# GpSimd makes three quarters of the first weight chunk's low halves, VectorE the rest in two pieces

## The chip, the cores and the metric

The kernel runs on one core of a Trainium2 chip. The metric is the device time of one execution in microseconds (us), smaller is better. The kernel before takes 1351.69 us, the median of three runs between 1349.7 and 1352.07 us.

## What is computed

Two transformer-like blocks over 256 positions of width 1024. The first block (gated linear attention beside sparse attention, then a mixture of 16384 experts with 128 chosen per position) ends in a residual sum; the second block opens with a norm and a wide projection.

```python
x = x + gate2 * _peer(h2, ...)          # end of the first block
return _rmsnorm(x, final_norm_g)
...
h = rmsnorm(x, g_mix[i])                # start of the second block
z = jnp.einsum("bsd,dn->bsn", h, w_in[i])
```

The change lies at this seam, in the product `z`.

## The kernel before, in words

**High and low halves.** A product of two 32-bit matrices is made of three passes of TensorE over rounded operands. A weight chunk `whole` is copied by ScalarE into a rounded tile `hi`, and VectorE makes `lo = whole - hi`. The activation is parted likewise (`h_hi` by ScalarE, `h_lo` by VectorE). The passes are hi by h_hi, hi by h_lo and lo by h_hi (`three`, lines 770, 771, 772).

**The chunks of z.** The weights of `z` come in 9 chunks of 128x4096 elements: 8 blocks k of 512 columns, one for each 128 rows of the width. Chunk 0 (`FIRST_C`) is loaded by SyncE in four quarters of 1024 columns (two blocks k each), the others whole. `low` of a chunk lies where `whole` of it lay (`w_lo` is an alias of `raw`), so each subtraction reads and writes in place; both of its inputs are in SBUF.

**Order of work at the seam.** Each engine runs its own stream in order, written out by hand; semaphores join them.

- VectorE: the last two expert rows are added to the sum (`last_row`, four instructions of 128x512), then `expert_x(1, k)` adds the transposed expert sum of the second 128 positions to `xT` (128x128, one input from PSUM, one from SBUF), and `low_of_x(k)` makes `h_lo` of block k (128x256, two inputs from SBUF, line 1917) followed by `expert_x(1, k + 2)`. Between these, `rest_first(q)` (line 2509) makes the low halves of quarter q of chunk 0. After block 7, `rest()` (line 1959) makes the low halves of chunk 1.
- ScalarE: `part_first` (line 1353) rounds quarters 0 and 1 of chunk 0; then for each k it waits for `expert_x(1, k)` and makes `h_hi` of block k (`hi_of_x`, line 1356), with quarters 2 and 3 after k = 1 and 2, and from k = 3 on a square of 128x128 behind each. After k = 7 come three more squares (line 1726) and `part()` (line 1346), the rounding of chunk 1.
- TensorE: `turn_experts(1)` transposes the expert sum (L1093), with unread matmuls between (L1169), and `first_gate` does the 96 matmuls of chunk 0, four banks abreast, block k by block k. Its k = 0 stands on lines 1179 (high by high), 1182 (high by low) and 1185 (low by high); each later k waits for `h_lo` of that block, and k = 2, 4, 6 for the low halves of the next quarter. Then come 16 matmuls of sums of squares (line 1198) and chunk 1 on lines 770 to 772, which waits for the low halves of all of chunk 1.
- GpSimd: it issues the gathers of expert rows (lines 659 and 664). After the last of them its stream is empty.

The semaphore `w_hi` counts rounded chunks and quarters, `w_lo` the low halves made by VectorE; `split_count` gives the count that belongs to a chunk and block.

Of the kernel before, what the change touches and what calls it, by code (L numbers as in the profile page):

```python
# [14 lines left out]
F32 = mybir.dt.float32  # L15
U32 = mybir.dt.uint32
F32R = mybir.dt.float32r
ALU = mybir.AluOpType
# [7 lines left out]
KD = D // P  # L26
# [128 lines left out]
FIRST_C = CHUNK_AT[("z", 0)]  # L155
FIRST_B = BLOCK_AT[("z", 0)]
WHOLE = ("iq", "yb", "ya")
PARTED = [n for n, c in enumerate(CHUNKS) if c[0][0] not in WHOLE]
PARTED_EARLY = len([key for key in EARLY if key[0] not in WHOLE])
# [3 lines left out]
PG = CHUNK_AT[("pg", 0)]  # L163
# [33 lines left out]
def halves(stage, k=0):  # L197

    names = [name for name, _ in HALVES]
    return sum(n for _, n in HALVES[:names.index(stage)]) + k + 1  # L200
# [10 lines left out]
def split_count(c, k=KD - 1):  # L211

    n = PARTED.index(c)
    if n < PARTED_EARLY:
        return n + 1
    at = n + 1 + (k // 2 if n == PARTED_EARLY else KD // 2 - 1)
    return at + (k // 4 if c == PG else n > PARTED.index(PG))


INPUTS = ["dsa_w_uv", "gla_w_gate_up"]  # L220
# [2 lines left out]
def two_blocks(nc, w, out):  # L223
    with ExitStack() as ctx:
        made = {}

        def S(name):

            if name not in made:
                made[name] = ctx.enter_context(nc.semaphore(name))  # L230
            return made[name]
# [32 lines left out]
        def alias(name, start, *dims, dt=F32R):  # L264

            pad = [(name + "_pad", [P, start], F32)] if start else []
            return overlay(*pad, (name, [P, *dims], dt))[-1]
# [30 lines left out]
        def again(start, *dims):  # L298

            at[0] = start  # L300
            return view(*dims)
# [112 lines left out]
        raw, w_lo = again(a_raw, SLOTS, W), alias("w_lo", a_raw, SLOTS, W)  # L414
# [6 lines left out]
        w_hi = alias("w_hi", a_ring, SLOTS, W)  # L421
# [30 lines left out]
        def parts(c):  # L452

            n = CHUNKS[c][2] * CHUNKS[c][5]
            if c in PQ_HOME:
                where, lo, hi, _, _ = PQ_HOME[c]
                return pq_raw[where][:, lo, 0:n], pq_r[where][:, hi, 0:n], pq_r[where][:, lo, 0:n]
            if c < FIRST_C:
                r = c % RAW
                return e_raw[:, r, 0:n], e_hi[:, c % 3, 0:n], e_lo[:, r, 0:n]  # L460
            r, h = (c - FIRST_C) % SLOTS, -(PARTED.index(c) - PARTED_EARLY) % SLOTS
            hi = first_hi if c == FIRST_C else w_hi[:, h, :]
            return raw[:, r, 0:n], hi[:, 0:n], w_lo[:, r, 0:n]

        def by_block(a, n=512):
            return a.rearrange("p (k n) -> p k n", n=n)
# [11 lines left out]
        def quarter(a, q):  # L478
            return a[:, q * QUARTER:(q + 1) * QUARTER]
# [239 lines left out]
            head(N_HEAD - 1, 1, last=True)  # L719


        @block.tensor
        def _(pe):
            done = [0]

            def begin(key):

                n = BLOCK_AT[key]
                assert n == done[0], (key, n, done[0])
                done[0] += 1  # L730
                c = chunk_of(n)
                if key[0] == "down":
                    pass
                elif key[0] == "pl":
                    pe.wait_ge(S("p_in"), 32)
                elif c in PARTED:

                    if c == FIRST_C:
                        pe.wait_ge(S("w_hi"), split_count(c, 0))
                    else:  # L740
                        pe.wait_ge(S("w_lo"), split_count(c, 0 if c == PG else KD - 1))
                else:
                    pe.wait_ge(*arrival(c))
                if BANK_BEFORE[n] is not None:

                    e = BLOCKS[BANK_BEFORE[n]][1]
                    pe.wait_ge(S("taken_" + e), taken_by(e, BANK_BEFORE[n]))
                if key[0] == "pl":
                    return BK[BANK_OF[n]], ple_w
                if c in PARTED:  # L750
                    return BK[BANK_OF[n]], None
                _, _, kt, _, _, nn = CHUNKS[c]
                whole = e_raw[:, c % RAW, 0:kt * nn] if c < FIRST_C else raw[:, (c - FIRST_C) % SLOTS, 0:kt * nn]
                return BK[BANK_OF[n]], whole.rearrange("p (k n) -> p k n", n=nn)
# [23 lines left out]
            def abreast(name, m, x_hi, x_lo, stage, between=None, after=KD - 2, n=T):  # L778


                outs = [begin((name, b))[0][:, 0:n] for b in range(m)]
                for k in range(KD):
                    pe.wait_ge(S("x_lo"), halves(stage, k))
                    if name == "pg" and k == 4:
                        pe.wait_ge(S("w_lo"), split_count(PG, k))
                    for b in range(m):
                        mm = three(outs[b], (name, b), column((name, b)), k, x_hi, x_lo)
                        if k == KD - 1:
                            mm.then_inc(S("product"), 1)
                    if between and k == after:  # L790
                        between()
# [381 lines left out]
            def first_gate():  # L1173

                outs = [begin(("z", b))[0][:, 0:T] for b in range(4)]
                hi, lo = (by_block(a) for a in parts(FIRST_C)[1:])
                pe.wait_ge(S("x_hi"), halves("z", 0))
                for b in range(4):
                    pe.matmul(outs[b], hi[:, 0, b * P:(b + 1) * P], h_hi[:, 0, :], start=True, stop=False, skip_group_check=True)
                pe.wait_ge(S("x_lo"), halves("z", 0))  # L1180
                for b in range(4):
                    pe.matmul(outs[b], hi[:, 0, b * P:(b + 1) * P], h_lo[:, 0, :], start=False, stop=False, skip_group_check=True)
                pe.wait_ge(S("w_lo"), split_count(FIRST_C, 0))
                for b in range(4):
                    pe.matmul(outs[b], lo[:, 0, b * P:(b + 1) * P], h_hi[:, 0, :], start=False, stop=False, skip_group_check=True)
                for k in range(1, KD):
                    pe.wait_ge(S("x_lo"), halves("z", k))
                    if k in (2, 4, 6):
                        pe.wait_ge(S("w_lo"), split_count(FIRST_C, k))
                    for b in range(4):  # L1190
                        mm = three(outs[b], ("z", b), b * P, k, h_hi, h_lo)
                        if k == KD - 1:
                            mm.then_inc(S("product"), 1)
# [53 lines left out]
            for j in range(4):  # L1247
                outs = [begin(("down", 2 * j + b))[0] for b in range(2)]
                for half in range(2):
                    c = CHUNK_AT[("down", j, half)]  # L1250
                    pe.wait_ge(S("w_lo"), split_count(c))
                    hi, lo = (by_block(a, 256) for a in parts(c)[1:])
                    for b in range(2):
                        o, cs = outs[b][:, 0:T], slice(b * P, (b + 1) * P)
                        for k in range(FB // 2):
                            f = half * FB // 2 + k
                            if j == 0 and b == 0:

                                pe.wait_ge(S("f_lo"), f + 1)
                            pe.matmul(o, hi[:, k, cs], f_hi[:, f, :], start=f == 0, stop=False, skip_group_check=True)  # L1260
                            pe.matmul(o, hi[:, k, cs], f_lo(f), start=False, stop=False, skip_group_check=True)  # L1261
                            mm = pe.matmul(o, lo[:, k, cs], f_hi[:, f, :], start=False, stop=f == FB - 1,  # L1262
                                           skip_group_check=True)
                        if half:
                            mm.then_inc(S("product"), 1)
                    if half == 0:
                        mm.then_inc(S("down_half"), 1)
# [639 lines left out]
        def _(v):  # L1907
# [594 lines left out]
            link(v.tensor_tensor(g2e[:, :], cols("final_norm_g", KD), cols("final_norm_g", KD), ALU.mult))  # L2502
            link(v.tensor_scalar(g2e[:, :], g2e[:, :], EPS, None, ALU.add))

            def rest_first(q):

                whole, hi, lo = (quarter(a, q) for a in parts(FIRST_C))
                v.wait_ge(S("w_hi"), split_count(FIRST_C, 2 * q))
                v.tensor_tensor(lo, whole, hi.bitcast(F32), ALU.subtract).then_inc(S("w_lo"), 1)

            link(v.tensor_scalar(half_id[:, 0, :], rowid[:, 1, LAST_J - 1:EK], 1, None, ALU.logical_shift_left))
# [31 lines left out]
            def low_of_x(k):  # L2543
                lo_of_x("z", k, gfm[:, k:k + 1])
                if k + 2 < KD:
                    expert_x(1, k + 2)

            low_of_x(0)
            for q in range(4):
                rest_first(q)  # L2550
                for k in (2 * q + 1, 2 * q + 2):
                    if k < KD:
                        low_of_x(k)
            rest()
            v.wait_ge(S("nm_root"), 1)
            link(v.reciprocal(stat[:, 1, :], tmp))
# [298 lines left out]
```

## Time and profile before

| | |
|---|---|
| median of 3 runs | 1351.69 us |
| profiled execution, its own time | 1353.7 us |
| its span | 1352.0 us |
| TensorE busy, share of the span | 90% |
| VectorE / ScalarE / GpSimd busy | 78% / 46% / 21% |
| mean granted TensorE clock | 0.986 |
| the seam, from the last expert matmuls to chunk 1 of z | some 963 to 984 us from the start |

The profiled execution took 1353.7 us, which is its span of 1352.0 us and 1.7 us around it. Times in the rows are from the start of the span. A row of the timeline gives start, length, engine, line, operation, written tile, read tiles, shapes, and in brackets how long the engine was idle before it and what ended that. The engines' names are PE (TensorE), PEld (its weight loads), DVE (VectorE), ACT (ScalarE) and POOL (GpSimd).

### The profile page before, as it was taken

The numbers are of one execution on the slowest core, as the hardware profiler recorded it, in microseconds if no ns is written. First come the engines' busy times: TensorE is split into PE (matmuls) and PEld (weight loads), VectorE is DVE, ScalarE is ACT, GpSimd is POOL, SyncE is SP. The second block draws the span as 40 slices with busy tenths as digits, with TensorE's granted clock in tenths as the row PEclk, the third lists the DMA queues.
The fourth block names the chain that finished last, engine by engine and source line by source line (L and its number), as shares of the span: only waits on it lengthen the run. The fifth ranks groups of instructions, "written<-read, shape, count | busy, mean of one in ns | idle before, by whom it ended". The sixth has DMA issues, their size and how long they took to land. (4 is left out here: it accounts for less than half of the span.)

```text
span 1352.0 us, 19494 instructions
## 1 busy us (share of the span) xinstructions
PE 1215.2 (90%) x6952; PEld 908.0 (67%) x6952; DVE 1059.7 (78%) x2161; ACT 616.0 (46%) x1265; POOL 290.1 (21%) x280
## 2 busy tenths in 40 slices
PE   7999999999989877778877777787899999999998
PEld 5999999999743333324332232333699999999998
DVE  7898678887879777777766777777699978898666
ACT  4666555656333333332433333233563265554445
POOL 1010000002545544344444434443000000000000
PEclk9999999999999999999999999999999999999999
DMA  9966446665999999999999999999853545454461
GB/s 388 384 225 249 187 158 235 245 234 234 375 422 426 427 428 428 427 427 427 427 427 427 427 428 428 428 427 428 341 187 126 187 137 183 180 187 173 174 236 43
DMA packets 55488, 416.64 MB, mean 308 GB/s; under 512 B 6113, under 2 KB 6753, under 8 KB 9202
## 3 DMA queue, kind: packets, MB, share of 16 engines
q0 software_dynamic: 37152, 268.45, 47.2%
q1 hardware_dynamic: 17792, 146.51, 29.3%
q8 instruction: 50, 0.82, 0.2%
q10 hardware_dynamic: 466, 0.63, 0.1%
q14 instruction: 28, 0.23, 0.0%
HBM read 414.52 MB, written 1.05 MB: 307 GB/s over the span
## 5 line engine op out<-in xcount | busy, mean ns | idle before, releaser
L1109 PE MATMUL ps<-arena 128*128 128x512 f32 x512 | 234.6, 603 | 57.0 <-ACT arena L1613 57.0
L1109 PE MATMUL ps<-ring,arena 128*128 128x512 f32 x440 | 214.1, 637 | 47.1 <-ACT arena L1613 47.1
L2377 DVE CUSTOM_DVE_ANT_0 arena<-arena 128x1024 f32<-128x1024 f32 x128 | 151.7, 1223 | 99.0 <-DMA arena<-in_experts,rowid 96.3
L1109 PEld LDWEIGHTS ps<-arena 128*128 128x128 f32 x512 | 92.7, 189 | 193.9 <-ACT arena L1613 98.0
L659 POOL DMA_INDIRECT arena<-in_experts,rowid x128 | 128.7, 1005 | 351.7 <-DVE rowid L2304 191.0
L1109 PEld LDWEIGHTS ps<-ring,arena 128*128 128x128 f32 x440 | 86.1, 202 | 170.4 <-issue 92.6
L772 PE MATMUL ps<-h_hi,w_lo 128*128 128x256 f32 x700 | 194.9, 278 | 0.0
L1606 ACT ACTIVATE arena<-arena 128x2 f32<-128x2 f32 x126 | 25.6, 203 | 369.1 <-DVE arena L2377 368.9
L770 PE MATMUL ps<-h_hi,w_hi 128*128 128x256 f32 x672 | 189.0, 281 | 3.0 <-DVE w_lo L1959 2.4
L771 PE MATMUL ps<-h_lo,w_hi 128*128 128x256 f32 x672 | 187.2, 279 | 0.0
L2377 DVE CUSTOM_DVE_ANT_0 ring<-ring,arena 128x1024 f32<-128x1024 f32 x112 | 133.3, 1222 | 35.4 <-DMA ring<-in_experts,rowid 26.5
L659 POOL DMA_INDIRECT ring<-in_experts,rowid x110 | 127.1, 1155 | 133.2 <-PE ps L1109 98.9
L1959 DVE TENSOR_TENSOR w_lo<-arena,w_hi 128x4096 fp32r<-128x4096 f32 (+1 forms) x30 | 122.1, 4069 | 29.7 <-ACT w_hi L1346 29.1
L1346 ACT ACTIVATE w_hi<-arena 128x4096 fp32r<-128x4096 f32 (+1 forms) x30 | 100.4, 3346 | 76.2 <-DMA arena<-in_up_w 32.1
L772 PEld LDWEIGHTS ps<-h_hi,w_lo 128*128 128x128 f32 x700 | 132.3, 189 | 0.0
L770 PEld LDWEIGHTS ps<-h_hi,w_hi 128*128 128x128 f32 x672 | 127.3, 190 | 4.1 <-DVE w_lo L1959 3.0
L771 PEld LDWEIGHTS ps<-h_lo,w_hi 128*128 128x128 f32 x672 | 127.1, 189 | 0.2
L770 PE MATMUL ps<-n_hi,e_hi 128*128 128x256 f32 (+1 forms) x352 | 101.4, 288 | 0.2 <-issue 0.2
L771 PE MATMUL ps<-n_lo,e_hi 128*128 128x256 f32 (+1 forms) x352 | 98.1, 279 | 0.0
L772 PE MATMUL ps<-n_hi,e_lo 128*128 128x256 f32 (+1 forms) x352 | 98.1, 279 | 0.0
L1959 DVE TENSOR_TENSOR e_lo<-ring,e_hi 128x2048 fp32r<-128x2048 f32 (+1 forms) x38 | 86.3, 2271 | 11.4 <-ACT e_hi L1346 10.8
L1613 ACT ACTIVATE arena<-ident,arena 128x128 f32<-128x128 f32 x252 | 85.4, 386 | 0.0
(424 smaller groups left out, 2558.4 us busy)
## 6 DMA issues: line engine op xcount, KB each, us to landing
ring<-in_early_w SPq DMA_DIRECT2D x43, 1024.0 KB, 5.0
arena<-in_ada_w SPq DMA_DIRECT2D x24, 1024.0 KB, 8.1
arena<-in_up_w SPq DMA_DIRECT2D x11, 2048.0 KB, 7.8
arena<-in_z_w SPq DMA_DIRECT2D x8, 2048.0 KB, 7.9
arena<-in_down_w SPq DMA_DIRECT2D x8, 1408.0 KB, 6.1
arena<-in_o_w SPq DMA_DIRECT2D x2, 2048.0 KB, 8.1
arena<-in_early_w SPq DMA_DIRECT2D x3, 1024.0 KB, 7.6
arena<-in_experts,rowid POOLq DMA_INDIRECT x128
```

What stands on the lines that cost most here:

```text
L659: pool.indirect_dma_start(out=rows[j], out_offset=None, in_=w["experts"], in_offset=bass.IndirectOffsetOnAxis(ap=rowid[:, even, j:j + 1], ...
L770: pe.matmul(out, hi[:, k, c0:c0 + m], x_hi[:, k, :], start=k == 0, stop=False, skip_group_check=True)
L771: pe.matmul(out, hi[:, k, c0:c0 + m], x_lo[:, k, :], start=False, stop=False, skip_group_check=True)
L772: return pe.matmul(out, lo[:, k, c0:c0 + m], x_hi[:, k, :], start=False, stop=k == KD - 1, skip_group_check=True)
L1109: mm = pe.matmul(BK[4 + 2 * t + b], diag[:, j, :], rows[j][:, D + b * 512:D + (b + 1) * 512], start=first and j == 0, stop=last and j == ( ...
L1346: act.activation(hi, whole, ACT.Copy).then_inc(S("w_hi"), 1)
L1606: act.activation(gel[:, even, two], dots[:, even, two], ACT.Gelu).then_inc(S("act_head"), 1)
L1613: act.activation(diag[:, j, :], ident[:, :], ACT.Copy, scale=amul[:, even, j:j + 1]).then_inc(S("diag"), 1)
L1959: v.tensor_tensor(lo, whole, hi.bitcast(F32), ALU.subtract).then_inc(S("w_lo"), 1)
L2377: v.tensor_tensor_reduce(out=u, in0=u, in1=h2tok[:, t, :], scale=1.0, scalar=0.0, op0=ALU.mult, op1=ALU.add, accum_out=dots[:, even, j:j + ...
```

## The change

GpSimd gets three subtractions behind its last gather: the low halves of quarters 1, 2 and 3 of chunk 0, each after the rounding of its quarter, counted on a new semaphore `first_lo`. VectorE makes quarter 0 only, in two pieces of 512 columns (blocks 0 and 1), each ahead of the `low_of_x` of the next block. TensorE waits for `w_lo` at k = 0 and 1 and for `first_lo` at k = 2, 4, 6. `low_count` corrects the later counts of `w_lo` by two.

```diff
+def low_count(c, k=KD - 1):
+
+    n = PARTED.index(c)
+    if n == PARTED_EARLY:
+        return n + 1 + k
+    return split_count(c, k) - (2 if n > PARTED_EARLY else 0)
...
             head(N_HEAD - 1, 1, last=True)
+            whole, hi, lo = parts(FIRST_C)
+            for q in (1, 2, 3):
+                pool.wait_ge(S("w_hi"), split_count(FIRST_C, 2 * q))
+                pool.tensor_tensor(quarter(lo, q), quarter(whole, q), quarter(hi, q).bitcast(F32), ALU.subtract
+                                   ).then_inc(S("first_lo"), 1)
...
-                pe.wait_ge(S("w_lo"), split_count(FIRST_C, 0))
+                pe.wait_ge(S("w_lo"), low_count(FIRST_C, 0))
...
                 for k in range(1, KD):
                     pe.wait_ge(S("x_lo"), halves("z", k))
+                    if k == 1:
+                        pe.wait_ge(S("w_lo"), low_count(FIRST_C, k))
                     if k in (2, 4, 6):
-                        pe.wait_ge(S("w_lo"), split_count(FIRST_C, k))
+                        pe.wait_ge(S("first_lo"), k // 2)
...
-            def rest_first(q):
-
-                whole, hi, lo = (quarter(a, q) for a in parts(FIRST_C))
-                v.wait_ge(S("w_hi"), split_count(FIRST_C, 2 * q))
+            def rest_first(k):
+
+                whole, hi, lo = (by_block(a)[:, k, :] for a in parts(FIRST_C))
+                v.wait_ge(S("w_hi"), split_count(FIRST_C, 0))
                 v.tensor_tensor(lo, whole, hi.bitcast(F32), ALU.subtract).then_inc(S("w_lo"), 1)
...
             low_of_x(0)
-            for q in range(4):
-                rest_first(q)
-                for k in (2 * q + 1, 2 * q + 2):
-                    if k < KD:
-                        low_of_x(k)
+            for k in range(1, KD):
+                if k <= 2:
+                    rest_first(k - 1)
+                low_of_x(k)
             rest()
```

VectorE's stream at the seam before, from the `h_lo` of block 0 to the second quarter (L1917 on `h_lo` is `low_of_x`, on `xT` it is `expert_x`, L2509 is `rest_first`; two more such rounds follow):

```order
L1917 SCALAR_TENSOR_TENSOR h_lo<-xT,mod,h_hi 128x256
L1917 SCALAR_TENSOR_TENSOR xT<-ps,adaT,xT 128x128
L2509 TENSOR_TENSOR w_lo<-arena,first_hi 128x1024
L1917 SCALAR_TENSOR_TENSOR h_lo<-xT,mod,h_hi 128x256
L1917 SCALAR_TENSOR_TENSOR xT<-ps,adaT,xT 128x128
L1917 SCALAR_TENSOR_TENSOR h_lo<-xT,mod,h_hi 128x256
L1917 SCALAR_TENSOR_TENSOR xT<-ps,adaT,xT 128x128
L2509 TENSOR_TENSOR w_lo<-arena,first_hi 128x1024
```

and after the change, from the same instruction on (the lines are 17 further down):

```order
L1934 SCALAR_TENSOR_TENSOR h_lo<-xT,mod,h_hi 128x256
L1934 SCALAR_TENSOR_TENSOR xT<-ps,adaT,xT 128x128
L2526 TENSOR_TENSOR w_lo<-arena,first_hi 128x512
L1934 SCALAR_TENSOR_TENSOR h_lo<-xT,mod,h_hi 128x256
L1934 SCALAR_TENSOR_TENSOR xT<-ps,adaT,xT 128x128
L2526 TENSOR_TENSOR w_lo<-arena,first_hi 128x512
L1934 SCALAR_TENSOR_TENSOR h_lo<-xT,mod,h_hi 128x256
L1934 SCALAR_TENSOR_TENSOR xT<-ps,adaT,xT 128x128
```

The second piece now stands ahead of block 2 instead of ahead of block 3, both pieces are half as wide, and only `h_lo` and `xT` instructions follow up to chunk 1. The end of GpSimd's stream after the change (before, it ends with the gathers):

```order
L667 DMA h_rows<-in_experts,rowid 128x2048
L667 DMA ring<-in_experts,rowid 128x2048 x5
L672 DMA ring<-in_experts,topu 128x1024 x4
L733 TENSOR_TENSOR w_lo<-arena,first_hi 128x1024 x3
L232 UNCONDITIONAL_BRANCH
```

The three subtractions are the only instructions added to GpSimd, and nothing is queued behind them.

## Rows read from the trace of the kernel before

**Rows 1.** The page: busy time and share of the span by engine.

```profile
PE 1215.2 (90%) x6952; PEld 908.0 (67%) x6952; DVE 1059.7 (78%) x2161; ACT 616.0 (46%) x1265; POOL 290.1 (21%) x280
```

**Rows 2.** Waits of TensorE, 984 to 1060, then 1060 to 1150: total, times, longest.

```profile
PE ps L770 <- DVE w_lo L1959: 0.5, 1, 0.5
...
PE ps L770 <- DVE xT L2675: 0.6, 1, 0.6
```

**Rows 3.** Timeline of TensorE at the seam: start us, length us, instruction.

```profile
967.92 0.71 PE L1179 MATMUL ps<-h_hi,first_hi 128*128 128x256 f32 x4
...
970.15 0.28 PE L770 MATMUL ps<-h_hi,first_hi 128*128 128x256 f32 x1
...
972.10 0.36 PE L770 MATMUL ps<-h_hi,first_hi 128*128 128x256 f32 x1 [0.43 <-DVE w_lo L2509]
...
980.35 3.61 PE L1198 MATMUL ps<-arena,csil 128*128 128x256 f32 x16
984.44 0.39 PE L770 MATMUL ps<-h_hi,w_hi 128*128 128x256 f32 x1 [0.47 <-DVE w_lo L1959]
```

**Rows 4.** The chain that ended last, at the seam: start us, length us, engine.

```profile
974.79 0.27 DVE xT L1917
...
975.51 0.90 ACT arena L1726 x4
976.40 3.54 ACT w_hi L1346
979.96 4.43 DVE w_lo L1959
```

**Rows 5.** Timeline of VectorE at the seam.

```profile
966.71 0.74 DVE L1917 SCALAR_TENSOR_TENSOR arena<-ring,arena 128x512 f32<-128x512 f32 x1
...
967.63 0.48 DVE L1917 SCALAR_TENSOR_TENSOR h_lo<-xT,mod,h_hi 128x256 fp32r<-128x256 f32 x1
968.04 0.35 DVE L1917 SCALAR_TENSOR_TENSOR xT<-ps,adaT,xT 128x128 f32<-128x128 f32 x1
968.30 1.22 DVE L2509 TENSOR_TENSOR w_lo<-arena,first_hi 128x1024 fp32r<-128x1024 f32 x1
969.43 0.48 DVE L1917 SCALAR_TENSOR_TENSOR h_lo<-xT,mod,h_hi 128x256 fp32r<-128x256 f32 x1
```

**Rows 6.** Timeline of ScalarE at the seam: quarters 0 and 1, then quarter 2.

```profile
964.99 2.21 ACT L1353 ACTIVATE first_hi<-arena 128x1024 fp32r<-128x1024 f32 x2 [1.86 <-DMA arena<-in_z_w]
...
968.17 1.04 ACT L1353 ACTIVATE first_hi<-arena 128x1024 fp32r<-128x1024 f32 x1
```

**Rows 7.** Timeline of VectorE: a subtraction's like of 512 columns.

```profile
998.47 0.69 DVE L2474 TENSOR_TENSOR arena<-arena 128x512 f32<-128x512 f32 x1
```

**Rows 8.** Timeline of GpSimd: instructions that read SBUF, in order.

```profile
1.25 0.28 POOL L628 TENSOR_SCALAR_AFFINE_SELECT ident<-ident 128x128 f32<-128x128 f32 x1 [0.24 <-POOL ident L627]
...
57.24 2.33 POOL L648 TENSOR_SCALAR_AFFINE_SELECT arena<-arena 128x128 f32<-128x128 f32 x1 [52.40 <-DVE arena L1917]
...
97.38 2.44 POOL L651 TENSOR_SCALAR_AFFINE_SELECT arena<-arena 128x256 f32<-128x256 f32 x1 [12.74 <-DVE arena L2037]
134.22 1.09 POOL L654 TENSOR_SCALAR_AFFINE_SELECT arena<-arena 128x1024 f32<-128x1024 f32 x1 [34.41 <-ACT arena L1492]
```

**Rows 9.** Timeline of VectorE at two of these moments.

```profile
57.12 2.29 DVE L1959 TENSOR_TENSOR e_lo<-ring,e_hi 128x2048 fp32r<-128x2048 f32 x1
...
97.27 2.29 DVE L1959 TENSOR_TENSOR e_lo<-ring,e_hi 128x2048 fp32r<-128x2048 f32 x1
```

**Rows 10.** Busy by stretch, 1159 to 1165: length, engines, granted clock, DMA share, GB/s.

```profile
1159.00:1160.00 1.00, 0.00 (x0) 0.00 (x0) 1.00 (x2) 0.56 (x1) 0.00 (x0) 1.00 1.42 229
1160.00:1161.00 1.00, 0.91 (x6) 0.91 (x7) 1.00 (x4) 0.00 (x0) 0.00 (x0) 0.83 0.48 164
...
1162.00:1163.00 1.00, 1.00 (x6) 1.00 (x6) 0.96 (x3) 0.00 (x0) 0.00 (x0) 0.50 0.99 426
...
1164.00:1165.00 1.00, 1.00 (x10) 1.00 (x9) 0.43 (x1) 0.53 (x2) 0.00 (x0) 0.96 0.88 377
```

More of the change, by code:

```diff
@@ L740, in begin @@
                     else:
-                        pe.wait_ge(S("w_lo"), split_count(c, 0 if c == PG else KD - 1))
+                        pe.wait_ge(S("w_lo"), low_count(c, 0 if c == PG else KD - 1))
                 else:
@@ L784, in abreast @@
                     if name == "pg" and k == 4:
-                        pe.wait_ge(S("w_lo"), split_count(PG, k))
+                        pe.wait_ge(S("w_lo"), low_count(PG, k))
                     for b in range(m):
@@ L1250, in _ @@
                     c = CHUNK_AT[("down", j, half)]
-                    pe.wait_ge(S("w_lo"), split_count(c))
+                    pe.wait_ge(S("w_lo"), low_count(c))
                     hi, lo = (by_block(a, 256) for a in parts(c)[1:])
```

## The prediction

> **What bounds the kernel now.** The page's shares come first: TensorE is busy 90% of the span [rows 1]. TensorE's own waits say where anything else decides: from 984 to 1150 us it waits 1.1 us in all [rows 2], so what the seam gains or loses passes on nearly whole to that stretch and, since loads there start when products end, past it. The measure of this change is therefore one number, the start of chunk 1 on TensorE, now 984.44 us [rows 3].
>
> Two chains end there. The chain of waits goes from VectorE's last `expert_x` at 974.79 over ScalarE's squares and its rounding of chunk 1 (976.40) to VectorE's subtraction (979.96 to 984.39) [rows 4]. TensorE's own stream is close behind: chunk 0 and the sums of squares end some 0.5 us before the wait does [rows 3]. In it, block 1 starts at 970.15, blocks 2 to 7 take from 972.10 to 980.35, which is 1.375 us for a block, and the second quarter's low halves cost one stall of 0.43 us [rows 3].
>
> **What is removed and added, were nothing in the way.** VectorE loses four subtractions of 1024 columns. One delays the next instruction by 1.13 us (968.30 to 969.43 [rows 5]), so 4.5 us go. It gains two of 512 columns, a like of which took 0.69 us [rows 7], some 0.62 us each to the next one. An `h_lo` takes 0.41 us to the next start and an `expert_x` 0.26 [rows 5]. ScalarE loses nothing, but its last h_hi could come earlier: with the last `expert_x` no longer behind four subtractions it would be bound by its own work, and the rounding of chunk 1 could begin near 974.3 instead of 976.4, the low halves end near 982.3. TensorE then starts block 1 at about 970.25 (after the second piece: 968.30 + 0.62 + 0.41 + 0.26 + 0.62), loses the 0.43 us stall, ends block 7 at 970.25 + 7 x 1.375 = 979.9 and the 16 matmuls at 979.9 + 3.61 = 983.5. Gain: 984.44 - 983.5 = 0.9 us, TensorE's stream being late next. More than 2.1 us, what ScalarE gives back, isn't to be had at all.
>
> **What GpSimd pays.** The trace has no two-input instruction on GpSimd. The nearest row is a one-input one of 1024 columns, 1.09 us [rows 8]. Lower end: the second input is free, 1.1 us. If the inputs are read one after the other, 2.2 us. Upper end, three such passes with the write: 3.3 us. I take 2.2, since GpSimd walks its elements for each operand. GpSimd's stream is otherwise empty, nothing waits behind it, and three of 2.2 us would be in time for blocks 2, 4 and 6 if they ran freely: quarter 1 is rounded at 967.2 [rows 6], so they would end at 969.4, 971.6 and 973.8, against needs at 971.6, 974.4 and 977.1. The Trainium skill ("GPSIMD Engine Reference", section Performance versus the Vector engine) has a two-input instruction of 2048 columns at 4497 ns, by which ours would be an estimated 2.25 us; no row here shows one.
>
> **What they do to each other.** This decides. A select of 128x128 takes 0.28 us alone. The same shape issued at 57.24 took 2.33 us and ended at 59.57, just after VectorE's two-input subtraction of 57.12 to 59.41; a 128x256 one issued at 97.38 ended at 99.82, after the subtraction of 97.27 to 99.56 [rows 8, 9]. (A third pair at 81.9 is the same.) So GpSimd doesn't read SBUF beside a VectorE instruction with two SBUF inputs: it waits for its end. The reverse order occurs nowhere in this trace. A port that one of them holds for an instruction should block the other in both directions, and then the price is this, with 2.2 us each:
>
> - GpSimd is released at 967.2, waits for the last expert row (966.71 + 0.74 [rows 5]) and runs 967.45 to 969.65. `low_of_x(0)`, which ran at 967.63, waits until 969.65.
> - VectorE's `low_of_x(0)` ends at 970.05, `expert_x` (one SBUF input) runs free; GpSimd takes the gap: quarter 2, rounded by 969.2 [rows 6], from 970.1 to 972.3. The first piece waits until 972.3 and ends at 972.95.
> - `low_of_x(1)` to 973.35; GpSimd takes the next gap: quarter 3, 973.4 to 975.6. (ScalarE rounded it after `expert_x` of block 2, near 971.9.) The second piece runs 975.6 to 976.25.
> - Block 1 on TensorE starts at 976.25 instead of 970.15, ends block 7 at 976.25 + 9.6 = 985.85, the 16 matmuls at 989.45. The other chain: `expert_x` of block 7 ends near 978.9 (3.8 us late), chunk 1's low halves near 988.4. TensorE decides: 989.45 - 984.44 = **+5.0 us**.
>
> Should GpSimd hold on from quarter 1 to 2 without letting VectorE in between, the same walk gives +4.3. With 1.1 us an instruction the sum falls to about +1.3, with 3.3 it grows to about +8.5.
>
> The Trainium skill ("SBUF — State Buffer", section Who interferes with whom) speaks against this change: a VectorE instruction with two SBUF inputs and a GpSimd one that reads SBUF shut each other out for a whole instruction, whichever began first. By that rule the sum is the +5.0 above, and without it the -0.9. The trace agrees in one direction, with 2.33 us for 0.28 [rows 8]; for the other no row speaks.
>
> **The clock.** In this case TensorE has from 968.5 to 976.25 only 8 matmuls, some 1.2 us of work. After 1158.2 it stood still for 1.9 us, and the granted clock went from 1.00 to 0.50 (2.4 to 1.2 GHz) at about 1160.8 and back before 1164.1: 0.17 + 3 x 0.50 + 0.04 = 1.7 us lost [rows 10]. Gaps of 1.6, 2.2 and 2.8 us in a row should bring one such drop while block 1 and the following run. Lower end 0, upper end twice as much, 3.4. I take **+1.7 us**.
>
> Sum: +5.0 + 1.7 = +6.7 us. The profiled time of 1353.7 would become 1360.4; it lies 2.0 us above the median of 1351.69, which becomes **1358.4 us** (+0.5%).
>
> **Rivals.** A (forecast), mutual blocking: 0.62. Its own range is 1354.5 to 1361.5: 1.2 us of port time less or more, with and without the drop.
>
> B, not slower: the two engines don't block each other while GpSimd is the one that holds. For it: no row shows VectorE waiting for GpSimd's reads, and all needs of blocks 2, 4 and 6 are then met with 2 us to spare. Against it: [rows 8, 9]. It decides if a two-input VectorE instruction that starts during a subtraction of GpSimd keeps its length (0.48 us for an `h_lo`). Then -0.9 us: 1350.8, at most -2.1. Chance 0.18.
>
> C, VectorE is never held up but GpSimd is: it gets only the `expert_x` slots (six of 0.26 us) until VectorE runs out of work near 973.5, so quarter 1 ends near 974.1, 2 near 976.3, 3 near 978.5 or behind chunk 1's subtraction. Block 2 would start at 974.1 instead of 971.6, the end of the 16 matmuls be 974.1 + 6 x 1.375 + 3.61 = 986.0: +1.5 us, 1353.2; if quarter 3 falls behind chunk 1's subtraction, +5. Chance 0.20.
>
> That the change doesn't move the work is excluded by the order of the streams; that GpSimd comes late to it is not likely, as its last gather is issued long before the seam.
>
> **How the numbers follow.** A run of this kernel can tell about 0.2% from no change, 2.7 us. Of A, 0.58 is slower by more than that and 0.04 within it (a short port time, no drop). Of C, 0.04 is slower, 0.16 within. Of B, 0.14 is within; 0.04 I leave to faster, for a gain that the bound of 2.1 us and the spread of runs of 1 us together could show. That makes 0.62 slower, 0.34 the same, 0.04 faster. The range takes in A but its upper tail, C, and the upper part of B: 1351.2 to 1360.8 us.
>
> **What would show it.** Right: `h_lo` or the 512-column pieces show lengths of 2 us or more (or starts that late) while GpSimd subtracts; GpSimd's three last 2.2 to 3 us each and lie interleaved with them; block 1 starts near 976; the granted clock shows 0.50 for some 3 us behind it; chunk 1 starts 5 to 7 us later. Wrong: `h_lo` instructions of 0.48 us inside GpSimd's subtractions. If GpSimd's are stretched to 3 us and more while VectorE keeps its lengths, it is C. Wrong in size only: a port time far from 2.2 us, or no drop of the clock.

## The result and the profile after

The changed kernel takes 1357.85 us (median of 8 runs, 1357.22 to 1365.7); the kernel before took 1351.3 in its 8 runs beside them. The medians differ by 6.5 us. The ratio of all these runs is 1.0058 with a 95% interval of 1.0046 to 1.0069, which is 7.8 us (two runs of the change took 1361.72 and 1365.7 us and pull it up). Slower either way. The profiled execution took 1358.04 us, its span 1356.3.

VectorE's timeline at the seam, in the changed kernel (columns as before; 17 lines further down than before):

```profile
962.66 0.75 DVE L1934 SCALAR_TENSOR_TENSOR arena<-ring,arena,ps 128x512 f32<-128x512 f32 x1 [1.51 <-ACT arena L1701]
...
966.22 2.32 DVE L1934 SCALAR_TENSOR_TENSOR h_lo<-xT,mod,h_hi 128x256 fp32r<-128x256 f32 x1
968.45 0.34 DVE L1934 SCALAR_TENSOR_TENSOR xT<-ps,adaT,xT 128x128 f32<-128x128 f32 x1
968.72 2.58 DVE L2526 TENSOR_TENSOR w_lo<-arena,first_hi 128x512 fp32r<-128x512 f32 x1
971.22 2.57 DVE L1934 SCALAR_TENSOR_TENSOR h_lo<-xT,mod,h_hi 128x256 fp32r<-128x256 f32 x1
973.72 0.34 DVE L1934 SCALAR_TENSOR_TENSOR xT<-ps,adaT,xT 128x128 f32<-128x128 f32 x1
973.98 0.68 DVE L2526 TENSOR_TENSOR w_lo<-arena,first_hi 128x512 fp32r<-128x512 f32 x1
974.58 0.47 DVE L1934 SCALAR_TENSOR_TENSOR h_lo<-xT,mod,h_hi 128x256 fp32r<-128x256 f32 x1
```

GpSimd's timeline there, its second and third subtraction (the first runs from 965.87 for 2.38 us):

```profile
968.20 2.55 POOL L733 TENSOR_TENSOR w_lo<-arena,first_hi 128x1024 fp32r<-128x1024 f32 x1
...
970.71 2.80 POOL L733 TENSOR_TENSOR w_lo<-arena,first_hi 128x1024 fp32r<-128x1024 f32 x1
```

Three VectorE instructions with two SBUF inputs last 2.3 to 2.6 us where their like take 0.47 and 0.68 in the same rows (0.48 in [rows 5], 0.69 in [rows 7]); each ends 0.3 to 0.6 us after a subtraction of GpSimd does, which is no more than its own undisturbed length. The second and third subtraction of GpSimd, for their part, begin while a VectorE instruction of this kind is running, and end 2.21 us after it has ended (968.54 and 971.30). The `expert_x` at 968.45, one input of which is in PSUM, keeps its 0.34 us, though it lies wholly inside GpSimd's second subtraction. Once GpSimd is done, at 973.5, every length is as before.

TensorE's timeline (answers to [rows 3]):

```profile
968.59 0.74 PE L1197 MATMUL ps<-h_lo,first_hi 128*128 128x256 f32 x4 [1.38 <-DVE h_lo L1934]
971.35 1.22 PE L1200 MATMUL ps<-h_hi,w_lo 128*128 128x256 f32 x4 [2.03 <-DVE w_lo L2526]
974.80 0.55 PE L785 MATMUL ps<-h_hi,first_hi 128*128 128x256 f32 x1 [2.23 <-DVE w_lo L2526]
...
980.04 0.28 PE L785 MATMUL ps<-h_hi,first_hi 128*128 128x256 f32 x1
...
986.85 3.61 PE L1215 MATMUL ps<-arena,csil 128*128 128x256 f32 x16
990.11 0.47 PE L785 MATMUL ps<-h_hi,w_hi 128*128 128x256 f32 x1
```

and the granted clock, in stretches of 1 us (columns as in [rows 10]):

```profile
969.00:970.00 1.00, 0.32 (x3) 0.12 (x1) 1.00 (x1) 1.00 (x2) 1.00 (x1) 0.89 0.99 426
...
973.00:974.00 1.00, 0.00 (x0) 0.00 (x0) 1.00 (x3) 0.00 (x0) 0.51 (x1) 0.50 1.18 508
...
976.00:977.00 1.00, 1.00 (x6) 1.00 (x6) 1.00 (x4) 1.00 (x4) 0.00 (x0) 0.50 0.08 33
...
980.00:981.00 1.00, 1.00 (x11) 1.00 (x10) 0.00 (x0) 1.00 (x1) 0.00 (x0) 0.99 0.00 0
```

TensorE waits 5.6 us in block 0 (1.38, 2.03 and 2.23). Its granted clock falls at about 969.8 and stays at 0.50 to 980.0, and its first 24 matmuls from block 1 on take 5.24 us where 24 take 2.7 at full clock (0.34 for three, as from 980.04 on).

**A measure for the seam.** The expert phase ahead of the seam differs by a few us between executions (its end is 1.4 us earlier in this one), so all traces are compared by one length: from VectorE's first `last_row` instruction (the `arena<-ring,arena,ps` row above, 964.09 before) to the first matmul of chunk 1. Before: 984.44 - 964.09 = 20.35 us. After: 990.11 - 962.66 = 27.45, **7.1 us more**.

### The profile page after: what moved, and what is told of

The parts are those of the page before. It is cut to its first block and busy times, and to the rows that moved or that the text cites. A ratio compares the mean times of both kernels' runs of the same rounds, so it can differ in the third digit from the quotient of the medians.

```text
span 1356.3 us, 19496 instructions
## 1 busy us (share of the span) xinstructions
PE 1218.3 (90%) x6952; PEld 910.7 (67%) x6952; DVE 1062.9 (78%) x2159; ACT 617.2 (46%) x1265; POOL 298.4 (22%) x283
## 5 line engine op out<-in xcount | busy, mean ns | idle before, releaser
L1976 DVE TENSOR_TENSOR w_lo<-arena,w_hi 128x4096 fp32r<-128x4096 f32 (+1 forms) x30 | 122.1, 4069 | 29.4 <-ACT w_hi L1363 28.8
L1976 DVE TENSOR_TENSOR e_lo<-ring,e_hi 128x2048 fp32r<-128x2048 f32 (+1 forms) x38 | 86.3, 2272 | 11.3 <-ACT e_hi L1363 10.7
```

## The experiments

The theories: (1) the engines shut each other out when both read SBUF, VectorE with two inputs; (2) the loss comes from the new order on VectorE; (3) they hinder each other only in the same tile; beside them the question whether the clock's drop is a price of its own. Single runs spread more here than in the first comparison (the kernel before between 1348.9 and 1360.19 us), so the seam's length carries more of the verdicts than the medians. The seam is from one profiled execution of each kernel; the ratios are against runs of the kernel before on the same chip.

| kernel | seam, us | against before | median, us | ratio (95%) |
|---|---|---|---|---|
| before | 20.35 | | 1351.30 to 1352.36 | |
| changed | 27.45 | +7.10 | 1357.85 | 1.0058 (1.0046 to 1.0069) |
| pieces | 20.40 | +0.05 | 1353.28 | 0.9997 (0.9972 to 1.0023) |
| ceiling | 19.18 | -1.17 | 1352.19 | 0.9996 (0.9973 to 1.0019) |
| beside_two | 24.85 | +4.50 | 1357.39 | 1.0040 (1.0018 to 1.0062) |
| beside_write | 20.36 | +0.01 | 1352.29 | 1.0006 (0.9991 to 1.0021) |
| beside_one | 21.98 | +1.63 | 1353.61 | 1.0011 (0.9996 to 1.0026) |
| q3_early | 22.50 | +2.15 | 1354.21 | 1.0020 (1.0007 to 1.0034) |
| q3_late | 20.89 | +0.54 | 1355.32 | 1.0021 (1.0003 to 1.0038) |
| warm | 27.49 | +7.14 | 1360.25 | 1.0059 (1.0035 to 1.0083) |
| warm_short | 25.04 | +4.69 | 1356.08 | 1.0046 (1.0026 to 1.0065) |
| alone_one | 20.35 | 0.00 | 1352.91 (one run) | |

### VectorE's half alone: pieces

```diff
-            for q in (1, 2, 3):
-                pool.wait_ge(S("w_hi"), split_count(FIRST_C, 2 * q))
-                pool.tensor_tensor(quarter(lo, q), quarter(whole, q), quarter(hi, q).bitcast(F32), ALU.subtract
-                                   ).then_inc(S("first_lo"), 1)
...
                 if k <= 2:
                     rest_first(k - 1)
+                if k in (3, 5, 7):
+                    rest_quarter(k // 2)
                 low_of_x(k)
```

> VectorE's half of the change alone: quarter 0 in two pieces, quarters 1 to 3 made by VectorE again, nothing on GpSimd. If the two engines shut each other out over SBUF (theory 1), this is the kernel before within 1 us (0.1 us more on VectorE). If the loss comes from the two pieces and the new wait of block 1 (theory 2), it is slower by several us.

The seam is that of before, 0.05 us more, and the time is no different within its interval of some 0.25%. Theory 2 is out: neither the two pieces nor block 1's wait costs anything to speak of.

### What there was to gain: ceiling

```diff
-            for q in (1, 2, 3):
-                pool.wait_ge(S("w_hi"), split_count(FIRST_C, 2 * q))
-                pool.tensor_tensor(quarter(lo, q), quarter(whole, q), quarter(hi, q).bitcast(F32), ALU.subtract
-                                   ).then_inc(S("first_lo"), 1)
...
-                        pe.wait_ge(S("first_lo"), k // 2)
+                        pe.wait_ge(S("w_hi"), split_count(FIRST_C, k))
+                        lo = hi
```

> The change without GpSimd's three subtractions: quarters 1 to 3 get no low halves, TensorE reads the high halves in their place (same number of matmuls, that part of the computation is left out). Theory 1: h_lo instructions are back at 0.48 us, block 1 starts some 6 us earlier than in the changed kernel, no clock drop, chunk 1 starts 0.9 us earlier than before: 1350.4 us (1349.2 to 1351.3). Theory 2: still slower than before.

The seam is 1.17 us shorter, with TensorE's own stream deciding: about the 0.9 us expected of the kernel in which nothing is in the way. So the work that the change takes off VectorE is worth 1.2 us at most, under 0.1% of the time, which the times can't show (interval 0.9973 to 1.0019).

### The same load beside the kernel before, in another tile: beside_two

```diff
             head(N_HEAD - 1, 1, last=True)
+            scratch = rows[8][:, 0:D]
+            pool.wait_ge(S("v_used"), (N_HEAD - 1) * EK + 10)
+            for q in (1, 2, 3):
+                pool.wait_ge(S("w_hi"), split_count(FIRST_C, 2 * q))
+                link(pool.tensor_tensor(scratch[:, :], scratch[:, :], scratch[:, :], ALU.subtract))
+            pool.sem_inc(S("beside"), 1)
...
+            act.wait_ge(S("beside"), 1)
             for i in range(2):
                 for n in range(PE_TAPS):
```

> The kernel before, plus three two-input subtractions of 1024 columns on GpSimd at the same three moments, on a dead row of the expert buffer that nobody else touches at that time; VectorE keeps all its work. Theory 1 (shared port): VectorE's h_lo and quarter subtractions are held up by 2 us three times, +6 us, and up to +8.5 with a clock drop. Theory 3 (the two engines hinder each other only because they work in the same tile and its neighbourhood): same as before.

VectorE's timeline there:

```profile
965.75 1.90 DVE L1924 SCALAR_TENSOR_TENSOR h_lo<-xT,mod,h_hi 128x256 fp32r<-128x256 f32 x1
967.57 0.34 DVE L1924 SCALAR_TENSOR_TENSOR xT<-ps,adaT,xT 128x128 f32<-128x128 f32 x1
967.83 2.65 DVE L2516 TENSOR_TENSOR w_lo<-arena,first_hi 128x1024 fp32r<-128x1024 f32 x1
970.41 2.11 DVE L1924 SCALAR_TENSOR_TENSOR h_lo<-xT,mod,h_hi 128x256 fp32r<-128x256 f32 x1
```

GpSimd works on a row of the expert buffer that VectorE doesn't touch, and again three instructions are held up, by 1.4, 1.4 and 1.6 us (1.90, 2.65 and 2.11 against 0.48, 1.22 and 0.48 in [rows 5]): together 4.5 us, the seam's +4.50. Theory 3 is out. It is less than the 6 expected: GpSimd's subtractions took only 1.9 us in the two cases where they didn't wait (the first two take 3.93 us together; why they are shorter here than the 2.4 on the weights wasn't tried), and they began 0.3 to 0.4 us ahead of the VectorE instruction that they held up. The clock dropped here too (0.50 from about 972.3 to 975.7), but TensorE's own stream still ends just before VectorE's subtraction for chunk 1 does (986.9 and 987.0), so the drop cost nothing at the seam.

### Writes only, and one input: beside_write, beside_one

Both edits are shown against beside_two.

```diff
-                link(pool.tensor_tensor(scratch[:, :], scratch[:, :], scratch[:, :], ALU.subtract))
+                link(pool.memset(scratch[:, :], 0.0))
+                link(pool.memset(scratch[:, :], 0.0))
```

> The kernel before, plus three times two memsets of 1024 columns on GpSimd (about 2 us at each of the three moments) on the dead row: GpSimd writes and reads nothing. If what the engines share is a read port, VectorE keeps its lengths and the time is that of before within 1 us. If GpSimd holds reads and writes whatever it does: +4 to +8 us, as with the two-input instructions.

Six memsets of 0.96 us lie beside VectorE's instructions (967.14 to 973.2), and not one of these is longer than before. What is shared is on the reading side.

```diff
-                link(pool.tensor_tensor(scratch[:, :], scratch[:, :], scratch[:, :], ALU.subtract))
+                link(pool.tensor_scalar(scratch[:, :], scratch[:, :], 1.0, None, ALU.mult))
+                link(pool.tensor_scalar(scratch[:, :], scratch[:, :], 1.0, None, ALU.mult))
```

> The kernel before, plus three times two one-input instructions (tensor_scalar) of 1024 columns on GpSimd on the dead row, some 1.1 us each. Read port: each holds up one two-input instruction of VectorE by up to 1 us, +3 to +6 us in all. If only two-input instructions of GpSimd hinder: same as before.

GpSimd's reads hinder VectorE here too, but by less than expected (+1.63 at the seam instead of 3 to 6). Five of GpSimd's six instructions took 2.8 to 2.9 us instead of 1.1. The first four held up one `h_lo` each, by only 0.5 to 0.6 us; the fifth met nothing. The third:

```profile
976.32 0.99 DVE L1925 SCALAR_TENSOR_TENSOR h_lo<-xT,mod,h_hi 128x256 fp32r<-128x256 f32 x1
977.24 0.34 DVE L1925 SCALAR_TENSOR_TENSOR xT<-ps,adaT,xT 128x128 f32<-128x128 f32 x1
977.50 1.21 DVE L2517 TENSOR_TENSOR w_lo<-arena,first_hi 128x1024 fp32r<-128x1024 f32 x1
```

```profile
975.89 2.90 POOL L724 TENSOR_SCALAR h_rows<-h_rows 128x1024 f32<-128x1024 f32 x1
```

The `h_lo` issued at 976.32 ends at 977.3 and not 976.8; the subtraction at 977.50 runs at full speed inside the same GpSimd instruction. So it keeps VectorE out for about its first 0.9 us and not for its length. The other direction shows on the sixth, issued 0.4 us after VectorE's long subtraction for chunk 1 (984.26 to 988.69):

```profile
984.68 6.64 POOL L725 TENSOR_SCALAR h_rows<-h_rows 128x1024 f32<-128x1024 f32 x1
```

It ends 2.63 us after that subtraction: GpSimd waited for all of it, with one input as with two.

### How long it is alone: alone_one

The edit is shown against beside_one.

```diff
-            for q in (1, 2, 3):
-                pool.wait_ge(S("w_hi"), split_count(FIRST_C, 2 * q))
-                link(pool.tensor_scalar(scratch[:, :], scratch[:, :], 1.0, None, ALU.mult))
-                link(pool.tensor_scalar(scratch[:, :], scratch[:, :], 1.0, None, ALU.mult))
+            pool.wait_ge(S("x_lo"), halves("z", KD - 1))
+            link(pool.tensor_scalar(scratch[:, :], scratch[:, :], 1.0, None, ALU.mult))
```

> The kernel before with a single one-input instruction of 1024 columns on GpSimd after VectorE's last h_lo, where VectorE idles for 3 us. If its 2.8 us beside VectorE were mostly waiting, it now takes 1.1 us as the select of 1024 columns did; if it is its own work, 2.2 us or more.

With VectorE idle beside it:

```profile
976.37 2.78 POOL L723 TENSOR_SCALAR h_rows<-h_rows 128x1024 f32<-128x1024 f32 x1 [40.45 <-DVE h_lo L1923]
```

It is its own work, then, and more than the two-input subtraction of the same width takes (2.40 in q3_late below). The select's 1.09 us [rows 8] is no guide to it.

### One quarter only, in and out of the way: q3_early, q3_late

In both GpSimd makes quarter 3 alone; q3_late has one more wait.

```diff
-            for q in (1, 2, 3):
+            for q in (3,):
                 pool.wait_ge(S("w_hi"), split_count(FIRST_C, 2 * q))
+                pool.wait_ge(S("x_lo"), halves("z", KD - 1))
...
                 if k <= 2:
                     rest_first(k - 1)
+                if k in (3, 5):
+                    rest_quarter(k // 2)
                 low_of_x(k)
```

> As the one before, but GpSimd starts quarter 3 as soon as it is rounded, beside VectorE's h_lo instructions. Theory 1: one collision: one instruction of VectorE lasts 2 us longer, less the 1.1 us saved: +1 us (0.3 to 2) against before, no clock drop. If the price of the change were all or nothing: +6.

> GpSimd makes only quarter 3, and waits until VectorE has made its last h_lo (quarter 0 in two pieces, 1 and 2 on VectorE). Theory 1: VectorE has no two-input instruction from there until chunk 1's subtraction 3 us later, so GpSimd's 2.2 us collide with nothing: h_lo stays at 0.48 us, time as before, -0.5 to +0.8 us. If GpSimd's work were dear in itself (a slow start, its semaphore): +2 us or more.

Early, one collision with VectorE's subtraction of quarter 1:

```profile
970.86 3.29 DVE L2532 TENSOR_TENSOR w_lo<-arena,first_hi 128x1024 fp32r<-128x1024 f32 x1
```

It takes 3.29 us instead of 1.21, and TensorE waits 2.26 us for it: +2.15 at the seam, 1.0020 in time. That is just past the upper end expected. What decides the start of chunk 1 here is the other chain, as in the kernel before: TensorE waits 0.15 us for VectorE's low halves of chunk 1 (L1976), which are late because the last `expert_x` is 2.15 us late (12.78 us after the first `last_row` instead of 10.63). The subtraction that VectorE no longer makes stood behind that `expert_x`, so saving it is no use. Late:

```profile
976.44 2.40 POOL L734 TENSOR_TENSOR w_lo<-arena,first_hi 128x1024 fp32r<-128x1024 f32 x1 [39.63 <-DVE h_lo L1935]
```

No VectorE instruction is lengthened. The seam is 0.54 us longer, as TensorE now waits 0.8 us for GpSimd at block 6. Its ratio of 1.0021 is 2.8 us, more than the seam shows and more than the 0.8 us expected at most; its runs spread widely (1350.6 to 1358.9) and the interval reaches down to 1.0003. The seam explains half a microsecond of it, and the rest stays open; in time the two variants can't be told apart. At the seam the same instruction on the same data costs 2.15 us or 0.5 by when it is issued.

### The clock: warm, warm_short

```diff
+            def more_unread(n):
+                for _ in range(n):
+                    pe.matmul(BK[0][:, 0:P], ones[:, :], ident[:, :], start=True, stop=True)
...
+                more_unread(5)
                 pe.wait_ge(S("x_lo"), halves("z", 0))
...
+                more_unread(8)
                 pe.wait_ge(S("w_lo"), low_count(FIRST_C, 0))
...
+                more_unread(8)
                 for k in range(1, KD):
```

This is the edit of warm_short, against the changed kernel; in warm the numbers are 10, 16 and 16.

> The changed kernel with 10, 16 and 16 unread matmuls where TensorE waits in block 0, so that it doesn't stand still. If the drop of the clock is a price of its own (2.5 us, by 24 matmuls that took 5.2 us from 974.8 to 980.0 instead of 2.7), the granted clock stays at 1.00 and the time falls from 1357.9 by 2.5 us less up to 0.5 for the added matmuls: 1355.6. If the drop is a symptom that costs nothing of its own: unchanged.

The granted clock stayed at 1.00, but the unread matmuls took 3.7 us in each of the two later stretches (0.24 us each, twice what I had reckoned), so block 1 started 2.5 us late and the seam was 27.49 again. Its ratio is that of the change (1.0059), which by the expectation would make the drop a symptom without a price. But from block 1 to chunk 1 it took 12.88 us instead of the 15.31 of the changed kernel, so the clock's 2.4 us came back and the late start used them up; hence the second:

> The changed kernel with 5, 8 and 8 unread matmuls in TensorE's three stretches of waiting (of 128 columns in 32 bits, 0.24 us each by the run with more of them; the first holds twice what was thought). They fit into the waits of 1.4, 2.0 and 2.2 us, so block 1 starts where it does in the changed kernel. If the clock's drop is a price of its own: granted clock 1.00, chunk 1 on TensorE 2.5 us earlier against the first last-row instruction of VectorE (25.0 us instead of 27.45), the time 2.5 us below the changed kernel's. If not: 27.4 and no difference.

```profile
974.95 0.36 PE L785 MATMUL ps<-h_hi,first_hi 128*128 128x256 f32 x1 [0.93 <-DVE w_lo L2533]
984.55 3.61 PE L1222 MATMUL ps<-arena,csil 128*128 128x256 f32 x16
987.82 0.47 PE L785 MATMUL ps<-h_hi,w_hi 128*128 128x256 f32 x1
```

```profile
976.00:977.00 1.00, 1.00 (x11) 1.00 (x11) 1.00 (x4) 1.00 (x5) 0.00 (x0) 1.00 0.12 49
```

VectorE's first `last_row` stands at 962.78 there, so block 1 starts after 12.17 us (12.14 in the changed kernel) and chunk 1 after 25.04: the clock stays up and gives back 2.4 us of the 7.1, with the three blockings on VectorE as long as before. In time its median is 4.7 us above that of its own kernel before, against 6.5 for the change; the intervals of the two ratios overlap, so the 2.4 us rest on the two traces and on the 12.88 us of warm, and the times only point the same way.

## Why the prediction was right

- **The mechanism (rival A).** As forecast, the two engines block each other in both directions, three times, and everything after follows. GpSimd's subtractions took 2.38 to 2.80 us, 2.40 with VectorE idle, and 2.21 behind the VectorE instruction that they waited for, against 2.2 taken. They held VectorE up by 1.8 to 2.1 us each. The Trainium skill ("SBUF — State Buffer", section Who interferes with whom) says that a VectorE instruction with two SBUF inputs contends with a GpSimd one that reads SBUF, and not with one that only writes it. The runs now agree in the direction for which no row of before spoke: 2.32 us for 0.48, and nothing for memsets. A hold for the whole instruction, which the prediction took from there, is right for the subtraction; for the one-input `tensor_scalar` the measurement decides otherwise (0.9 of 2.9 us). An estimate from the Trainium skill's 4497 ns for 2048 columns ("GPSIMD Engine Reference", section Performance versus the Vector engine) is 2.25 us for our 1024; the trace has 2.40.
- **The walk.** One handover went otherwise: the third subtraction got in between the first piece and the `h_lo` of block 1, which stand back to back, and not in the gap of the next `expert_x`. So `h_lo` was held up (2.57 us) and not the second piece. The sum is the same, since the same instructions follow one another either way: block 1 was forecast 976.25 - 964.09 = 12.16 us after the first `last_row` and started after 12.14. That they agree to 0.02 us is luck: the steps between are off by up to 0.7 us and cancel.
- **The 16 matmuls** from their start to chunk 1 take 3.26 us when nothing is waited for (986.85 to 990.11), not 3.61, which is the length of the last of them too: 0.35 less than the sum had. So TensorE's own stream in the kernel before was ready 0.8 us ahead of the wait's end and not 0.5, and the forecast gain without blocking should have been 1.25 us instead of 0.9; ceiling has 1.17.
- **The clock.** Forecast +1.7 within 0 to 3.4, by one drop that lasted some 3 us [rows 10]; it measured 2.4 (warm_short) to 2.5 (24 matmuls at half speed), because the clock was down for ten microseconds, and still for 5.2 of them after block 1 began. The term was right in kind, and 0.7 too small because the drop lasted three times as long as the one that it was taken from.
- **Sum.** 5.0 - 0.35 + 2.45 = 7.1 at the seam, 6.7 forecast: two errors of opposite sign, so part of the agreement of 1358.4 us with the 1357.85 measured is luck. The 6.5 us of the medians and the 7.8 of the ratio lie on both sides of the seam's 7.1. The two profiled executions differ by 4.3 us only: the changed one reaches the seam 1.4 us earlier and is 1.4 us shorter behind it, where TensorE's wait for VectorE near 1158 went from 1.9 to 1.4 us. How much of that is chance between executions wasn't tried.
- **Rival B** (no blocking) fell: `h_lo` doesn't keep its 0.48 us. Its value, -0.9, was close to the -1.17 of ceiling. **Rival C** (VectorE never held up) fell by the same rows.

## What to carry to other kernels

Work moved to an idle engine is free only if it doesn't read through the same door. Beside VectorE instructions with two SBUF inputs, a two-input subtraction on GpSimd cost VectorE nearly its whole length, on the weights as on an unrelated tile, so the 3.3 us of VectorE's time that were moved away came back as 5.8 us of waiting. Look for one row where the two meet (a GpSimd instruction stretched to the end of a VectorE one), and expect a price in the other direction too; how large it is depends on GpSimd's operation (a `tensor_scalar` held VectorE up by half a microsecond only). Where VectorE has nothing to do, only the wait for GpSimd itself is left: 0.5 us at the seam in q3_late, against 2.15 in q3_early. And when the waiting falls on a TensorE that would otherwise be busy, add what the lower clock costs afterwards: here a third of the loss.

## What was not expected of the hardware

- A one-input `tensor_scalar` of 128x1024 on GpSimd takes 2.78 us alone, longer than a two-input subtraction of that width (2.40), while a select of it took 1.09 [rows 8]. It kept VectorE out for about the first 0.9 us of its 2.9 only, yet had to wait for the whole of a VectorE subtraction itself. Why it takes so long afterwards stays open.
- GpSimd gets its turn even between two VectorE instructions that follow each other without a gap: its third subtraction, issued at 970.71 during VectorE's first piece, began its work when that piece ended at 971.30, ahead of the `h_lo` issued at 971.22, which had to wait for it. In beside_two the third one came in the same way (between the quarter subtraction at 967.83 and the `h_lo` at 970.41).
